# Joint attentions of a streaming encoder step: two query tiles per pass over the values, and keys turned inside their own buffer

## The reference

```
# B: 4 heads, two 64-wide queries and keys per head, 128-wide values, chunk-causal mask
scores = einsum('bthed,bshed->bhets', q2, k2) * SCALE
p = softmax(where(mask, scores, NEG_INF)); attn = p[:, :, 0] - lam * p[:, :, 1]
out = einsum('bhts,bshd->bthd', attn, v)
# C: 16 heads of 64; cq, ck are cumulative sums of log forget values, causal mask
scores = einsum('bthd,bshd->bhts', q, k) * SCALE + cq[..., None] - ck[..., None, :]
out = einsum('bhts,bshd->bthd', softmax(where(mask, scores, NEG_INF)), v)
```

## Time and profile before

| | us |
|---|---|
| median of three runs | 3855.59 |
| profiled execution | 3852.3 |
| its span (first to last instruction) | 3850.6 |
| PE busy | 3470.9 (90%) |
| DVE busy | 1623.8 (42%) |
| ACT busy | 1068.1 (28%) |
| granted share of PE's clock, mean | 0.943 |

### The profile page before, as it was taken

The page is one execution under the profiler, slowest core; times in us unless marked ns, Lnnn a source line. Parts: engine busy times, 40 slices in busy tenths (PEclk is TensorE's granted clock), DMA queues, the critical chain, the costliest instruction groups (busy, mean ns, idle before and its releaser), DMA issues. The chain is left out here.

```text
span 3850.6 us, 63167 instructions
## 1 busy us (share of the span) xinstructions
PE 3470.9 (90%) x25160; PEld 3003.2 (78%) x25160; DVE 1623.8 (42%) x2919; ACT 1068.1 (28%) x2130; POOL 256.6 (7%) x338
## 2 busy tenths in 40 slices
PE   8988588877999999996999689989979899999997
PEld 7866366666999999995899566666657799999997
DVE  5317466544334233336211265565543333333334
ACT  4215244333121111113221143344333211111211
POOL 2310000023000000004000000000003100000003
PEclk9999599988999999998999789999989899999999
DMA  5447598634111111103553888988842211111102
GB/s 171 120 138 162 143 284 271 222 140 131 44 33 35 52 44 33 54 22 124 144 173 105 213 242 255 276 257 256 276 156 104 77 54 44 33 54 37 40 22 104
DMA packets 421232, 495.33 MB, mean 129 GB/s; under 512 B 97968, under 2 KB 273616, under 8 KB 420880
## 3 DMA queue, kind: packets, MB, share of 16 engines
q1 hardware_dynamic: 421024, 492.45, 42.5%
HBM read 409.20 MB, written 84.10 MB: 128 GB/s over the span
## 5 line engine op out<-in xcount | busy, mean ns | idle before, releaser
L2426 DVE TENSOR_TENSOR f_gated<-f_gated,f_up 128x384 f32<-128x384 f32 x132 | 73.2, 555 | 741.2 <-ACT f_gated L2359 741.2
L2525 PE MATMUL f_gate<-m_ht_hi,f_w_hi 128*128 128x384 f32 x1056 | 355.3, 336 | 25.8 <-DVE f_w_lo L2418 25.8
L2450 DVE TENSOR_TENSOR f_y<-f_y,f_down 128x512 f32<-128x512 f32 x396 | 269.7, 687 | 229.4 <-PE f_down L2538 229.3
L2525 PE MATMUL f_gate<-m_ht_hi,f_w_lo 128*128 128x384 f32 x1056 | 354.9, 336 | 0.0
L2525 PE MATMUL f_gate<-m_ht_lo,f_w_hi 128*128 128x384 f32 x1056 | 354.8, 336 | 0.0
L2525 PE MATMUL f_up<-m_ht_hi,f_w_lo 128*128 128x384 f32 x1056 | 352.7, 334 | 0.0
L2525 PE MATMUL f_up<-m_ht_lo,f_w_hi 128*128 128x384 f32 x1056 | 352.7, 334 | 0.0
L2525 PE MATMUL f_up<-m_ht_hi,f_w_hi 128*128 128x384 f32 x1056 | 352.7, 334 | 0.0
L2538 PE MATMUL f_down<-f_wo_hi,f_act_hi 128*128 128x512 f32 x792 | 312.7, 395 | 10.6 <-DVE f_y L2450 9.3
L2538 PE MATMUL f_down<-f_wo_hi,f_act_lo 128*128 128x512 f32 x792 | 309.2, 390 | 0.0
L2538 PE MATMUL f_down<-f_wo_lo,f_act_hi 128*128 128x512 f32 x792 | 309.1, 390 | 0.0
(11 more groups left out here) (378 smaller groups left out, 6817.3 us busy)
## 6 DMA issues: line engine op xcount, KB each, us to landing
jc_kc<-in_cache_c_k SPq DMA_DIRECT2D x64, 1024.0 KB, 5.9
jc_vc<-in_cache_c_v SPq DMA_DIRECT2D x64, 1024.0 KB, 11.5
f_raw<-in_w_ffn_in SPq DMA_DIRECT2D x88, 512.0 KB
jb_kc<-in_cache_b_k SPq DMA_DIRECT2D x32, 1024.0 KB, 8.5
jb_vc<-in_cache_b_v SPq DMA_DIRECT2D x32, 1024.0 KB, 11.1
f_raw_o<-in_w_ffn_out SPq DMA_DIRECT2D x22, 1024.0 KB, 6.1
f_raw<-x SPq DMA_DIRECT2D x18, 512.0 KB, 4.1
abp_raw<-in_w_ab_in SPq DMA_DIRECT2D x32, 256.0 KB, 3.0
```

What stands on the lines that cost most here:

```text
L2426: dve.tensor_tensor(prod[:, b], silu[:, b], up[:, q, 0:gw], ALU.mult).then_inc(prod_done, 1)
L2450: dve.tensor_tensor(part, part, down[:, half, :], ALU.add).then_inc(added, 1)
L2525: last = pe.matmul(acc[:, q, 0:gw], a[:, s, k, u, :], b[:, k, token], start=(k == 0 and j == 0), stop=(k == KT - 1 and j == 2))
```

## The change

1. **Values as weights.** `attend(k)` serves two steps, 2k and 2k+1. For each key tile the values are the weights and the turned probabilities of both query tiles move (256 columns, or 128 where the tile belongs to the longer query tile alone). `pv` then has the value dimension in partitions. In `jc` (64 wide) even key tiles go to partitions 0 to 63 and odd ones to 64 to 127.
2. **Turning back.** ACT copies `pv` (256 columns) to `o_turn` (`copy_output`), PE turns it back into a ring slot (`turn_back`: two transposes in `jb`; in `jc` two products with `halves`, two stacked identities of 64, which add the column halves), and DVE scales from the slot (`output`), every second step. `invert` stands by itself.
3. **Copies.** All copies of turned prompt probabilities are ACT's. `probs` has two buffers.
4. **Keys.** `kc` holds two sets of 17 places. Keys load to places 1 to 16 and DVE turns each one place down, in place of `kt`. A stream's first four tiles are turned in steps 6 and 7 of the unit before, the rest two to a step. The decay rows are stored in the score's order by stage `c`, and load in long rows.
5. **Sample steps.** The sample maximum is split in two halves (steps 0 and 1) and a small joining minimum; the exponential is at step 2, the turning at steps 3 and 4, the product with the values at step 5, its scaling at step 6. Scores are exponentiated in place.
6. **Loads.** `load_keys(u+1)` is issued first in a unit, values of two heads in one load, queries of four streams at a time. At the start both heads' queries and keys go ahead, and PE no longer waits for `select` before its first product.

```diff
-                    dve.tensor_scalar(sum_s[:], sum_s[:], -1.0, None, ALU.mult).then_inc(sample_done, 1)
+                    dve.tensor_scalar(logf_s[:, 0:PAST].rearrange("p (a t r) -> p a t r", a=4, r=32),
+                                      sum_s[:, 0:PAST].rearrange("p (t a r) -> p a t r", a=4, r=32), -1.0, None,
+                                      ALU.mult).then_inc(sample_done, 1)
+                    dve.tensor_scalar(logf_s[:, PAST:], sum_s[:, PAST:], -1.0, None, ALU.mult).then_inc(sample_done, 1)
...
-    turns_at = ((0, 1, 2), (3, 4, 5), (6, 7, 8), (9, 10, 11), (12, 13), (14, 15), (), ())
-    probs_at = ((), (), (0, 1, 2), (3, 4), (), (), (), ())
+    probs_at = ((), (), (), (0, 1), (2, 3, 4), (), (), ())
+    pairs_p = steps // 2
     order = [3, 4, 2, 5, 1, 6, 0, 7]
...
-                use(("p", n, g), "dve" if (done + g) % 4 == 3 else "act")
+                use(("p", n, g), "act")
...
-                if s == 6:
-                    use(("ot", u - 1), "dve", 1 if diff else 2)
+            k = (S * u + s - 2) // 2
+            if s % 2 == 0 and 0 <= k < pairs_p:
+                use(("po", k), "dve", 2)
+            if 1 <= u <= U and s == 7:
+                use(("ot", u - 1), "dve", 1 if diff else 2)
...
-        probs, probs_t = st.sb("probs", [P, 3, PROMPT]), st.sb("probs_t", [P, 2, TILES_P, P])
+        probs, probs_t = st.sb("probs", [P, 2, PROMPT]), st.sb("probs_t", [P, 2, TILES_P, 2, P])
...
+            def load_keys(u):
+                if u >= 2:
+                    sp.wait_ge(s_done, 2 * (u - 1))
+                for x in range(parts):
+                    sp.dma_start(kc[:, u % 2, 1 + per * x:1 + per * (x + 1)],
+                                 k_cache[stream_of(u), x * span:(x + 1) * span, columns_of(u)].rearrange(
+                                     "(t p) c -> p t c", p=P)).then_inc(kc_loaded[u % 2 * parts + x], 16)
...
             load_qk(0)
+            load_qk(1)
             load_v(0)
-            load_q(0)
-            load_keys(0, 0)
...
-            else:
+            load_keys(0)
+            load_q(0)
+            sp.wait_ge(setup, 14)
+            if not diff:
                 sp.dma_start(later[:], row_mask).then_inc(later_loaded, 16)
-                sp.wait_ge(setup, 12)
...
-                load_bias(0)
-            load_keys(0, 1)
-            load_qk(1)
+            load_bias(0)
+            load_new_keys(0)
             load_v(1)
...
             for u in range(U):
+                done = S * (u // 2)
                 if u + 1 < U:
-                    if (u + 1) % STREAMS == 0:
-                        load_q((u + 1) // STREAMS)
+                    load_keys(u + 1)
                     load_bias(u + 1)
-                    for x in range(parts):
-                        load_keys(u + 1, x)
                     load_new_keys(u + 1)
-                load_values(u)
+                    if (u + 1) % 4 == 0:
+                        load_q((u + 1) // 4)
...
                 if u + 2 < U:
                     load_qk(u + 2)
-                    load_v(u + 2)
-                store(u)
+                load_values(u)
...
-            def attend(n):
-                if n >= steps:
+            def attend(k):
+                if not 0 <= k < pairs_p:
                     return
...
+                h, t = 2 * k // S, tile_at(2 * k)
+                wait_emptied([("p", n, g) for n in (2 * k, 2 * k + 1) for g in range(len(group_of_step[n % S]))])
+                if k >= 1:
+                    pe.wait_ge(o_copied, k)
+                first = 0 if diff else h % 2 * dv
+                for x in range(tile_at(2 * k + 1) + 1):
+                    part = 0 if diff else x % 2 * dv
+                    e = 0 if x <= t else 1
+                    last = pe.matmul(pv[part:part + dv, e * P:2 * P], vp[:, h // 2 % 2, x, first:first + dv],
+                                     probs_t[:, k % 2, x, e:2, :].rearrange("p e q -> p (e q)"),
+                                     start=(x < P // dv), stop=(x > tile_at(2 * k + 1) - P // dv), skip_group_check=True)
                 last.then_inc(pv_done, 1)
 
-            def score_group(u, first):
-                if first == 0:
+            def turn_back(k):
+                pe.wait_ge(o_copied, k + 1)
+                slot = ring_slot(("po", k))
+                for e in range(2):
+                    src = o_turn[:, e * P:(e + 1) * P]
+                    if diff:
+                        last = pe.transpose(slot[:, e * P:(e + 1) * P], src, ident[:])
+                    else:
+                        held = DH if tile_at(2 * k + e) == 0 else P
+                        last = pe.matmul(slot[:, e * DH:(e + 1) * DH], src[0:held], halves[0:held], start=True, stop=True)
+                last.then_inc(turn_done, 1)
+
+            def score_keys(u, pair):
...
+                if u == 0:
+                    pe.wait_ge(setup, 14)
+                    if not diff:
+                        pe.wait_ge(later_loaded, 80)
...
-            pe.wait_ge(setup, 12)
-            if not diff:
-                pe.wait_ge(later_loaded, 80)
+            pe.wait_ge(setup, 10)
...
+                    if n % 2 == 1:
+                        attend((n - 1) // 2)
+                    if 1 <= u <= U and s == 5:
                         attend_sample(u - 1)
                     if u < U and s >= 6:
-                        score_group(u, 2 * (s - 6))
+                        score_keys(u, s - 6)
+                    if n % 2 == 0:
+                        turn_back((n - 2) // 2)
+                    if 1 <= u <= U and s == 7:
+                        turn_output(u - 1)
...
+            def copy_output(k):
+                if not 0 <= k < pairs_p:
+                    return
+                act.wait_ge(pv_done, k + 1)
+                if k >= 1:
+                    act.wait_ge(turn_done, seq[("po", k - 1)] + 1)
+                act.activation(o_turn[:], pv[:, 0:2 * P], ACT.Copy).then_inc(o_copied, 1)
...
+                    if n % 2 == 0:
+                        copy_output((n - 2) // 2)
+                    copy_prompt(act, n + 1)
                     if u >= 1 and s == 0:
...
+                        copy_scores(u - 1, 1)
+                    if u >= 1 and s == 2:
+                        exponential_sample(u - 1)
+                    if u >= 1:
                         for gi in probs_at[s]:
                             copy_probs(act, "act", u - 1, gi)
...
+            def output(k):
+                if not 0 <= k < pairs_p:
+                    return
+                h, j, key = 2 * k // S, k % 4, ("po", k)
+                dve.wait_ge(turn_done, seq[key] + 1)
+                dve.wait_ge(inv_done, 2 * k + 2)
...
-                dve.transpose(kt[:, t, :], kc[:, t // per, t % per, :]).then_inc(kt_done, 1)
+                if u < U:
+                    dve.wait_ge(kc_loaded[u % 2 * parts + t // per], 16 * (u // 2 + 1))
+                    if u or t:
+                        dve.wait_ge(kt_done, parts * per * u + t)
+                    dve.transpose(kc[:, u % 2, t, :], kc[:, u % 2, t + 1, :]).then_inc(kt_done, 1)
+
+            def turn_ahead(u, t):
+                if u == 0 and t < parts * per:
+                    if t % 2 == 1 and t >= 2 * per:
+                        turn_keys(0, 2 * t - 15)
+                elif u < U or t >= parts * per:
+                    turn_keys(u + t // (parts * per), t % (parts * per))
 
...
-            copy_prompt(dve, "dve", 0)
-            dve.wait_ge(setup, 2)
             for u in range(U + 1):
                 for s in range(S):
                     n = S * u + s
-                    if u < U and s == 0:
+                    if n % 2 == 1:
+                        output((n - 3) // 2)
+                    maximum(n + 3)
+                    if 1 <= u <= U and s == 6:
+                        scale_output(u - 1)
+                    if u == 0 and 2 <= s < 6:
+                        turn_keys(0, 4 * s - 8)
+                        turn_keys(0, 4 * s - 7)
+                        turn_keys(0, 4 * s - 6)
+                    turn_ahead(u, 2 * s + 4)
+                    if u < U and s == 3:
+                        turn_new(u)
+                    if u < U and s == 4:
+                        if u == 0:
+                            dve.wait_ge(setup, 14)
                         blocks(u)
...
+                    if 1 <= u <= U and s == 0:
+                        maximum_sample(u - 1, 0)
+                    if 1 <= u <= U and s == 1:
+                        maximum_sample(u - 1, 1)
+                    if 1 <= u <= U and s == 3:
+                        inverse_sample(u - 1)
+                    invert(n)
+                    turn_ahead(u, 2 * s + 5)
+                    if 1 <= u <= U and s == 7:
+                        copy_out(u - 1)
```

(4 more changed lines are left out.)

309 lines of the change are left out of this document (143 added, 166 removed).

## The result

The changed kernel is slower. Twenty runs give a median of 3881.06 us (3863.34 to 3896.20), twenty of the kernel before 3854.59 (3845.39 to 3866.97). The ratio is 1.0066, with a 95% interval of 1.0053 to 1.0079. The prediction was 3834 us with a range of 3785 to 3876, so its sign was wrong too.

A forecast was written before the change was run, and what follows sets the result against it. PE was taken as the bound (busy 90% of the span). `jc` units -10, `jb` units +6, `jc` start -13, `jb` start -5 sum to -22 us against a median of 3855.6, giving 3834 us, range 3785 to 3876.

The forecast's parts named there:

- At nothing: Parts counted as zero: the decay rows' new order, the double keys' buffer, the longer rows of values and stores.
- DMA is not the bound: Per unit, transfers need 34 us, a floor beneath PE; so longer rows of values and stores bring nothing.
- the halves do not run side by side: Rival: `jc` pays `jb`'s product price, 2.7 us a unit, 40 over 15 units; 3874 us, chance 0.05.
- the slower one: Rival: ACT and DVE pace steps 0 to 5, clock falls in every unit; +40 us, 3895, chance 0.14.
- The one on the starts: Rival: the stage starts bring nothing because the first keys come no earlier; 3852 us, chance 0.09.
- The low clock: Unit's second part: 3.4 to 6.8 us at half clock, in seven units of ten, costing 1.6 us a unit.
- the quiet unit: A `jc` unit at full clock; the forecast's sum without its low clock gives 40.4 - 1.6 = 38.8 us.
- The signs of being wrong: A unit below 38.5 or above 42 us, PE waiting for keys' or values' DMAs, or first keys' scores still late.
- The starts: First keys' scores come earlier: `jc` about 40 us after its start against 52.9 (-13), `jb` 476 for 481.2 (-5).
- PE's stall in step 3: PE waits some 2.3 us from T+8.6 (T: unit's start) for the ring slot that DVE empties.
- The halves side by side: In `jc` the column halves of the value products overlap; a pair product takes 1.07 us.
- `jb`'s units and end: `jb` behind its start: longer pair products, cheaper turnings back, +0.8 us a unit, +6 over 7 units.

The follow-up runs named there:

- run 2: `qk_behind`: changed kernel with the loads of queries and keys of the next but one head issued behind the sample's cached values; 3852.24 us, ratio 0.9999.
- run 8: Kernel of run 2 with all key tiles of `jc`'s pair product in the same 64 array columns, nothing side by side; 3905.89 us, ratio 1.0134.
- run 1: The changed kernel again, no edit; 3883.02 us, ratio 1.0089.
- Run 9: Changed kernel with run 2's edit, DVE's key turnings spread anew, and another order of first loads in each joint stage; 3829.18 us, ratio 0.9931.
- pad64: Changed kernel with 64 small products (128 instructions) on PE at the start of `jc`; 3884.14 us, ratio 1.0057.
- run 11: Kernel before the change with 64 small products (128 instructions) on PE at the start of `jc`; 3907.17 us, ratio 1.0112, four runs.
- run 6: Changed kernel, each load of queries and keys issued as two of half the columns (2 KB rows, not 4 KB); 3857.27 us, ratio 1.0000.

## Why the prediction was wrong

**The step that failed** is "At nothing", with "DMA is not the bound" as its reason: it lists the keys' buffer and the longer rows, and the new order of the loads within a unit has no term at all. That order, in part 6 of the change, made the kernel slow, and it acts through no wait of mine. I asked of each load whether its data come late. I never asked what else goes through the same engines: PE's instructions. Undone, it gives back 29 to 31 us (run 2), the whole loss against the kernel before. No rival of mine has this mechanism. Two came near in time by luck: that the halves do not run side by side (3874, chance 0.05), which run 8 refutes, and the slower one (3895, chance 0.14), of which only more low clock than forecast was true, and that not in every unit. The one on the starts (3852) was nearly right on its own part, as below.

**The low clock** was mis-sized. The sum has 1.6 us a unit for it. The 14 units from 2235.55 to 2839.93 take 43.17 on the mean; 39.12 are the quiet unit, 0.9 the stops (12.9 / 14), and 3.1 are left for the clock, twice the term. In `qk_behind` the 14 units take 40.98, which leaves 1.8: the excess goes with the stops and with stretches of 14 and 20 us at half clock (37 in run 1) that begin at or close behind the product and last over the keys' scores. In all profiles together nine low stretches of over 13 us begin in `jc` away from its start and end, and each begins inside a stop or less than 2 us behind it; the profiles without a stop have none. Most stops draw none, so a stop is not enough. I took 6.8 us as the longest. The signs of being wrong named a unit above 42 us; they did not name the cause.

**The starts** were too high: -18 forecast, -3 measured. By the marks of the forecast, the first keys' scores of `jc` (2203.1) come 48.0 us after its start, not 40, before 52.9; those of `jb` (483.2) come 50.0, before 48.7. I counted the megabytes ahead of the keys, and not that DVE has to turn the new keys in step 3, whose small load stands last. Run 9 gets 9 of the missing 15 by that.

**What was right.** PE's stall in step 3: forecast from T+8.6 to T+10.9, behind DVE's output of pair 0; measured in the unit from 2605.79, 2.15 us from T+8.5 to T+10.7. The halves side by side: 1.22 us for forecast 1.07, where one half alone takes 2.09 in run 8. The rule of the Trainium skill on weight loads that the prediction weighs (TensorE: Matmul & The Clock Gate, Part 3, What overlaps and what doesn't) does not hold for these halves, by these two numbers. The quiet unit: 39.1 for 38.8. `jb`'s units and end: +8.1 for +6, of which 2.4 are stops; the parts of that sum were not measured one by one, so some of it may be luck. Take the stops away (run 2) and `jc` behind its first new frames' scores is 651.6 us for 654.5 before, -3 where -10 was forecast: a unit is 40.98 for 40.4, of which 0.3 is the quiet unit and 0.2 the clock.

## What to carry to other kernels

A reordered load costs nothing only if nothing else needs the DMA engines at that time, and PE's own instructions come through them: look for PE idle on "issue" inside a dense run of small instructions, look whether an instruction packet ends 1.2 to 1.6 us ahead of where it goes on, and keep bursts off that run. Before a difference of 1% is put down to a change, move the program by some hundred instructions: the kernel before lost 1.1% by that and the changed one nothing, so with both moved the changed one no longer looks slower (3884 and 3907; they ran on different chips and the intervals of their ratios overlap, so the order of the two can't be told), while the versions without the traffic stayed within 6 us. A sum over a periodic unit should carry the low clock as a range with a tail, since one low stretch in the wrong place cost 14 to 22 us here.

## What the runs showed of the hardware

- PE's instructions came in packets of 16384 bytes that took 0.9 to 1.4 us. With full engines none started for up to 27 us, and PE then stood up to 2.8 us in the profile of the changed kernel, 3.3 in that of run 1, 4.7 in that of `pad64`, until 1.2 to 1.6 us after the packet's end.
- The clock stayed at 1.2 GHz for 20 to 44 us while PE was busy nearly throughout (20.40 of 20.40 us above, 42.30 of 44.30 in run 11). These stretches span the keys' scores, which run on 32x32 tiles and took 7.1 us in place of 3.7 for each 64 records. In them being busy did not bring the clock back.
- Packets of 4 KB of the queries and keys took about 300 ns each, packets of 2 KB of the sample's keys about 85, and the same queries and keys in 2 KB (run 6) a median of 84. Half as long a row moved faster per byte, but it was no gain once the traffic lay elsewhere.
